# Bias of the prompt heads stored with a skewed pitch, and transposes in place of products with a reversed unit matrix

## The reference

```python
for window, dil in DILATIONS:                      # (128,1), (512,4), (2048,16)
    ...
    bias = jnp.transpose(rel_bias[t5_bucket(delta * dil)].astype(jnp.float32), (2, 0, 1))
    sc = jnp.einsum("brnqhe,brnkhe->brnhqk", qs, kk) * scale + bias
    sc = jnp.where(valid[None, None, :, None], sc, -jnp.inf)
    ...
    o = jnp.einsum("brnhqk,brnkhe->brnqhe", p / l, vv)
return combine_by_denominator(outs, lses).astype(dtype)
```

## Time and profile before

| | us |
|---|---|
| time, median of 3 runs | 1132.92 |
| lowest and highest run | 1131.44, 1135.62 |
| span of the profiled execution | 1133.0 |
| TensorE busy in it | 1048.4 |
| VectorE busy | 546.4 |
| ScalarE busy | 203.2 |
| GpSimd busy | 41.7 |

### The profile page before, as it was taken

The page is one execution under the profiler, slowest core; times in us unless marked ns, Lnnn a source line. Parts: engine busy times, 40 slices in busy tenths (PEclk is TensorE's granted clock), DMA queues, the critical chain, the costliest instruction groups (busy, mean ns, idle before and its releaser), DMA issues.

```text
span 1133.0 us, 17343 instructions
## 1 busy us (share of the span) xinstructions
PE 1048.4 (93%) x7193; PEld 585.1 (52%) x7193; DVE 546.4 (48%) x1075; ACT 203.2 (18%) x463; POOL 41.7 (4%) x39
## 2 busy tenths in 40 slices
PE   8999999999999999999999998999998869788887
PEld 3687776666666666677777542323332323222232
DVE  3775554665545556484624126435443434333432
ACT  1022103221212331312001111111111111111112
POOL 0030110001100000000000000000000000000000
PEclk9999999999999999999999999999999999999999
DMA  9899539989999999733857448999999999999996
GB/s 314 346 281 307 211 135 383 360 338 347 347 417 378 382 358 355 306 131 126 337 204 273 172 188 374 426 413 425 430 426 426 428 427 429 429 428 427 426 427 237
DMA packets 38981, 384.54 MB, mean 339 GB/s; under 512 B 4911, under 2 KB 7599, under 8 KB 10895
## 3 DMA queue, kind: packets, MB, share of 16 engines
q1 hardware_dynamic: 36336, 375.83, 82.7%
q0 software_dynamic: 1568, 5.62, 1.9%
q10 hardware_dynamic: 1008, 2.10, 0.6%
HBM read 375.63 MB, written 7.90 MB: 339 GB/s over the span
## 4 chain that ended last, share of the span: by engine, by line
PE 71%; DMA 17%; DVE 8%; ACT 2%; issue 2%; POOL 1%; SPq 0%; ACTq 0%; DVEq 0%; POOLq 0%
PE ps L619 24%; DMA arena<-w_gu 13%; PE ps L611 7%; PE ps L1088 6%; PE ps L1015 5%; PE ps L1126 4%; PE ps L1107 4%; DMA arena<-w_proj 4%; PE ps L812 4%; PE ps L601 3%; PE ps L779 3%; DVE cst L1894 1%; DVE cst L1827 1%; PE ps L1131 1%; PE ps L795 1%
## 5 line engine op out<-in xcount | busy, mean ns | idle before, releaser
L619 PE MATMUL ps<-arena 128*128 128x256 f32 x1456 | 332.9, 383 | 2.1 <-DVE arena L1431 1.7
L619 PEld LDWEIGHTS ps<-arena 128*128 128x128 f32 x1456 | 270.6, 190 | 52.0 <-issue 14.7
L1088 PE MATMUL ps<-arena,cst 128*32 128x512 f32 x1024 | 120.8, 606 | 30.2 <-DMA arena<-w_gu 28.5
L1894 DVE STREAM_TRANSPOSE cst<-ps 128x512 f32<-128x512 f32 x31 | 22.2, 717 | 173.5 <-PE ps L1015 173.5
L611 PE MATMUL ps<-arena 128*64 128x256 f32 x832 | 101.3, 386 | 0.0
L1015 PE MATMUL ps<-arena,cst 128*32 128x512 f32 (+1 forms) x768 | 93.3, 599 | 0.5 <-DVE cst L1823 0.5
L1088 PEld LDWEIGHTS ps<-arena,cst 128*32 128x32 f32 x1024 | 31.9, 111 | 114.6 <-issue 79.8
L1107 PE MATMUL ps<-arena,stat 128*32 128x512 f32 x512 | 64.8, 625 | 23.3 <-DVE stat L1898 23.2
L611 PEld LDWEIGHTS ps<-arena 128*64 128x64 f32 x832 | 55.1, 136 | 37.8 <-issue 14.2
L1924 DVE COPY arena<-ps 32x512 f32<-32x512 f32 x62 | 42.9, 691 | 41.9 <-PE ps L1107 40.6
L1404 DVE TENSOR_TENSOR arena<-arena 128x512 f32<-128x512 f32 x52 | 35.7, 687 | 53.1 <-PE ps L619 41.8
(11 more groups left out here) (284 smaller groups left out, 979.4 us busy)
## 6 DMA issues: line engine op xcount, KB each, us to landing
arena<-w_gu SPq DMA_DIRECT2D x64, 2048.0 KB, 29.3
arena<-w_dn SPq DMA_DIRECT2D x32, 2048.0 KB, 27.7
arena<-w_proj SPq DMA_DIRECT2D x43, 1024.0 KB, 7.9
arena<-kc SPq DMA_DIRECT2D x16, 2048.0 KB, 10.7
arena<-vc SPq DMA_DIRECT2D x16, 2048.0 KB, 9.0
arena<-w_o SPq DMA_DIRECT2D x16, 1024.0 KB, 4.9
arena<-kc SPq DMA_DIRECT2D x8, 1024.0 KB, 8.3
arena<-vc SPq DMA_DIRECT2D x8, 1024.0 KB, 9.4
```

The source lines that it names most:

```text
L619: last = mm(psum[:, regions(v)[j - 1]], left[a], right[:, a], start=first and opens and a == 0, stop=final and a == 1, skip_group_check=True)
L1088: last = mm(ps[g:g + 32, 0, :], xgT[:, s % 2, kt, :], w[:, k, :], start=kt < 4, stop=kt >= KT - 4)
```

## The change

The bias in DRAM gets one row for each head and each query of a tile: 16 x 128 rows of 383 distances, all 128 rows of a head with the same content, at a pitch of 385 elements (`SKEW + 1`). The read takes a row every 384 elements (`SKEW`), so partition i starts one element earlier within its row than partition i - 1 does: offset 385 i + (127 - i). This is a pattern that steps forward in DRAM and backward in the distance, so that partition i now holds the bias of query i. The queries need no turning over, and `turn` and `pair_turn` use `nc.tensor.transpose` with the unit matrix everywhere. The columns of `flip` in the constants keep their place under the name `slots` and are zero.

The write is still one DMA from GpSimd, of 16 partitions, each read 128 times. The read is still one DMA a head pair, of 2 x 128 rows of 1024 B. No instruction changes its place in any engine's order.

```diff
+SKEW, SKEWED = 384, 383
...
-        pm = field(cst, CST["flip"][0], 3, P)
+        pm = field(cst, CST["slots"][0], 3, P)
...
-                sp.dma_start(bias_p[p % 2], bass.AP(tensor=bias_d.tensor, offset=p * 2 * TABLE + DIST0 - 255,
-                                                    ap=[[1, P], [TABLE, 2], [1, 256]])).then_inc(bp_loaded[p % 2], 16)
+                sp.dma_start(bias_p[p % 2], bass.AP(tensor=bias_p_d.tensor, offset=2 * p * P * (SKEW + 1) + P - 1,
+                                                    ap=[[SKEW, P], [P * (SKEW + 1), 2], [1, 256]])).then_inc(bp_loaded[p % 2], 16)
...
-                    if kind in (1, 3) and m == P:
-                        last = mm(ps[:, 3 + n % 2, r0:r0 + m], src, c("flip"), start=True, stop=True)
-                    else:
-                        last = tr(ps[:, 3 + n % 2, r0:r0 + m], src, ident[0:m, 0:m])
+                    last = tr(ps[:, 3 + n % 2, r0:r0 + m], src, ident[0:m, 0:m])
...
-                        last = mm(ps[:, 3 + k, a:a + 128], sc_p[k][:, a:a + 128], c("flip"), start=True, stop=True)
+                        last = tr(ps[:, 3 + k, a:a + 128], sc_p[k][:, a:a + 128], ident)
...
-            pool.dma_start(bias_d, table[:, :]).then_inc(tab_out, 16)
+            pool.dma_start(bias_p_d.rearrange("(h q) n -> h q n", h=H)[:, :, 0:SKEWED],
+                           table[:, DIST0 - 255:DIST0 - 255 + SKEWED].unsqueeze(1).to_broadcast([H, P, SKEWED])).then_inc(tab_out, 16)
...
-    scratch = {"bias_d": ((H, TABLE), F32), "bias_q_d": ((P, PAST + NQ), F32)}
+    scratch = {"bias_p_d": ((H * P, SKEW + 1), F32), "bias_q_d": ((P, PAST + NQ), F32)}
```

More of the change, by code:

```diff
@@ L95 @@
 _at = 0
-for _n, _w in (("ident", 128), ("gx", 16), ("flip", 128), ("ones", 128), ("ltri", 128), ("iota", 64),
+for _n, _w in (("ident", 128), ("gx", 16), ("slots", 128), ("ones", 128), ("ltri", 128), ("iota", 64),
                ("gmix", 16), ("gmem", 16), ("bs", 4), ("bss", 4), ("gff", 16), ("wr", KT * 36), ("wst", 4 * 128), ("wsbd", 4 * 64),
@@ L121, in hybrid_step @@
                 relb_d, onehot_d, w_gu, w_dn, mst_d, o_y, o_k, o_v, o_va, o_mk, o_mv,
-                bias_d, bias_q_d):
+                bias_p_d, bias_q_d):
     with ExitStack() as ctx:
@@ L2021, in constants @@
     c["ident"][:] = np.eye(P)
-    c["flip"][:] = np.eye(P)[::-1]
     c["ones"][:] = 1
```

## The result

The changed kernel takes 1144.35 us (median of 4 runs, 1143.49 to 1148.24), the kernel before 1133.68 us on the same chip (4 runs). The ratio is 1.0107 with a 95% interval of 1.0084 to 1.0129: slower by 10.7 us between the medians, by 12 us by the ratio. The forecast was 1128.5 us, with a range up to 1141 and 0.17 on slower. The profiled execution of the changed kernel took 1148.24 us (span 1146.4); the other three had spans of 1141.6 to 1142.9, so 4 of its microseconds are its own. They are not explained here; its granted clock in 700 to 760 us was 0.94, against 0.97 in the trace of before.

A forecast was written before the change was run, and what follows sets the result against it. TensorE, busy 1048.4 of 1133.0 us, was taken as the bound, with the DMA-full start second. 1133.0 less 6.5 for transposes plus 2.0 for late weights gave 1128.5 us; range 1124.5 to 1141.

The forecast's parts named there:

- How it shares: Bias write beside weights at the start: queues take turns packet by packet, weights get about 255 GB/s, bias about 97.
- step (4): Weights at the start: x's last tile and the weights of 87.66 us follow 0 to 3 us late; 2 us taken.
- The TensorE part: Head-pair turns: 64 fp32 products become 64 transposes, saving 5.3 to 7.2 us, 6.5 taken.
- Size: Bias write: grows from 160 KB to 3.14 MB from the same 16 partitions, at least 31.7 us at 99 GB/s.
- Step (1): GpSimd's issue of the 2048-row bias write: about 3 us, hidden because it has nothing to do until 58.15 us.
- Steps (2) and (3): Bias flows from 44.4 to 77 us, eight row writes to 87.5; SyncE waits before L459 until about 88.
- Step (5): DMA engine time at the start: turns add 13 us, 5.5 and about 6 are absorbed, 1.5 us is left.
- Rival C: Start: short rows drain below 73 GB/s, SyncE stands at L459 and issues weights late; 1140.5 us at 65 GB/s; chance 0.16.
- Rival B: Bias write: one row a packet, bias about 63 GB/s beside weights, weights of 87.66 us 5 us late; 1131.5 us; chance 0.14.
- Rival D: Head-pair turns: a transpose costs a quarter of a product, 0.056 us, saving 10.7 us; 1124 to 1125 us; chance 0.02.

The follow-up runs named there:

- e1: Changed kernel with its 64 transposes taken back to products with the unreversed unit matrix, skewed write and read kept: 1151.56 us, ratio 1.0172 to the kernel before.
- e2: Kernel before with only its 64 products turned into transposes, old 160 KB bias write kept: 1127.22 us, ratio 0.9947.
- e6: Changed kernel with the bias write out of 16 partitions issued late, at 114.17 us, and window loads at step 31: 1143.91 us, ratio 1.0108 to the kernel before.
- e7: Changed kernel with the one write replaced by two, twice the rows at half the length, same source: 1145.96 us, ratio 1.0110 to the kernel before.
- e11: Changed kernel with GpSimd issuing the same narrow write only after the gains landed, behind weights 7 and 8: 1151.29 us, ratio 1.0174 to the kernel before.
- e5: Changed kernel with the bias window made in 128 partitions, written late, at 110.91 us, and window loads at step 31: 1126.26 us, ratio 0.9942 to the kernel before.
- e4: Changed kernel with the same narrow write issued by ScalarE on its hardware queue, not GpSimd's: 1142.91 us, ratio 1.0112 to the kernel before.
- e8: Changed kernel writing 64 copies of each head's window, not 128, with reads all from the first copy: 1133.90 us, ratio 1.0019 to the kernel before.
- e3: Changed kernel with the bias window made in and written from 128 partitions, not 16, same bytes, rows and addresses: 1129.11 us, ratio 0.9973 to the kernel before.
- e10: Changed kernel with the bias window made in and written from 64 partitions, same 3.1 MB: 1127.86 us, ratio 0.9949 to the kernel before.
- e9: Changed kernel with the one write replaced by 16 writes of 8 copies a head, issued back to back: 1140.05 us, ratio 1.0067 to the kernel before.

## Why the prediction was wrong

The prediction failed in **"How it shares"**, and through it in step (4). It said that the queues take turns packet by packet from the first packet on, so that the weights would get 255 GB/s beside the write. They got nothing for ten microseconds, and then 1.12 MB in 57 to 66 us, 124 GB/s. Step (4) sized the delay of the weights at 0 to 3 us and its cost at 2; they were 16 to 23 us late, and the write cost 18.75 us (e1).

The error was in which row I let speak for the sharing. The earlier trace rows are two queues with full rows of 128 partitions on one side and a store of 128 partitions on the other. The earlier trace rows are the narrow writes, and I used them only for their rate. Yet the group shows q0 alone: the view had no row for q1 in 62 to 67 us, although weights had been issued at 63.33 us. The answer for 62 to 67 us in the kernel before has this line too:

```profile
arena<-w_proj SPq DMA_DIRECT2D x1, 1024.0 KB, 10.9
```

A block that lands in 4.8 us elsewhere took 10.9 us beside 1 MB of narrow writes. The stand-still was in the trace of before, in small.

The steps in turn:

- *The TensorE part*, 5.3 to 7.2 us, 6.5 taken: right. Measured 7.2 (e1) and 5.6 (e2). Six transposes span 0.82 and 0.87 us where 0.83 to 0.95 were forecast. TensorE got no new wait for VectorE or ScalarE: from 170 to 478 us it waits for them 2.8 us in all, line by line as in the kernel before.
- *Size*: right. 100 GB/s and 36.6 us to landing; predicted 97 GB/s from 44.4 to 77 us, measured landing 78.3. The packets hold three rows (4596 B), not two; each takes about 0.70 us when the write is alone.
- *Step (1)*, the issue hidden behind idle time: right, and cheaper (1.05 us, not 3).
- *Steps (2) and (3)*: the eight writes landed by 90.3 us, predicted 87.5 to 88. But SyncE never stood at the sample heads' loads for them, since it was itself 17.6 us late there.
- *Step (4)*: wrong, as said. The weights of 44.40, 50.44 and 56.49 us were 16, 23 and 22 us late. I had looked for the damage at 84 to 106 us, at the end of the write; it fell at 56 to 85 us, at its start.
- *Step (5)*, the sum by engine time, agreed with (4) and misled. It counts how much time the engines must give in all, 1.5 us more than they had. It doesn't say in what order they give it, and the order made the cost.
- *Rival C* was on the right side and for another reason: it let the write drain too slowly and hold SyncE at the end. The write drained as fast as forecast. *Rival B*'s packets did not come either. *Rival D* is refuted by the spans: six transposes 0.82 and 0.87 us long, less the 0.27 of the last record, stand 0.11 to 0.12 us apart, not 0.056.

The Trainium skill ("DMA: Bandwidth & Descriptors", Queues, rings and completion order) says that an engine goes round its queues packet by packet. In this trace that holds from 57.5 us on; the queues of the changed kernel from 57 to 66 us:

```profile
q0 software_dynamic: 182, 0.84, 68.1%
q1 hardware_dynamic: 164, 1.12, 29.6%
```

For the ten microseconds ahead the trace differs, with 223 packets to none, and so does e6 with 220 to 19; the measurement decides. The Trainium skill ("DMA: Bandwidth & Descriptors", Back-pressure in remote DMA) says of another kind of transfer that stalled writes hold up an engine's other queues; whether what is seen here is of that kind no run shows.

What stays open is why the weights' queue stands still, and what the 1.4 to 1.5 MB (1.2 to 1.7 with e7 and e11, about 0.5 in the late writes of e5 and e6) are. It is not a number of rows (e7) or packets (e4), a share of the write (e8), a time (e3, e10) or GpSimd's queue (e4), and it is less when less was issued ahead (e9, e5, e6). A limit on what is already handed to the engines would fit most of these, but no run shows such a limit itself, and it says nothing of e6, where the weights move but get one packet in twelve.

## What to carry to other kernels

A large write out of few partitions holds up the loads issued behind it, also those of another queue: here those issued 3, 9 and 15 us behind it were 16 to 23 us late, while one issued 0.6 us ahead was not. The faster the source gave the bytes, the sooner the first of them landed (21.5 us at 100 GB/s from 16 partitions, 13.9 us at 207 from 64), so spread the source first and choose the place second, with a step of weights in hand. When you size the sharing of two queues, take a row in which the slow one is of the same kind, read which queues are missing from it, and look at the landing times of what was issued then; a sum of engine time does not tell who is served first. And a wait of TensorE of some microseconds is to be priced with the slow work behind it: here 13.7 us of waiting cost 18.8.

## What was not expected of the hardware

- One write from 16 partitions kept the weights' queue at zero for ten microseconds, while the queue view showed the DMA engines full (97.8%).
- Packets of the write held three rows of 1532 B, or (e7) six of 768 B, on GpSimd's queue, and one row on ScalarE's; the rate was about 100 GB/s in each case.
- SyncE's issue of the gains, right behind weights 7, took 4.29 us where it takes 0.43 in the kernel before; it took 1.21 us in e3, 2.41 in e10 and 4.31 in e4.
- An idle stretch of 9.6 us brought TensorE's granted clock to 0.50, and it was still 0.68 on average in 67 to 73 us.
